# A feed-forward stage in seven products: two weight buffers and four hidden buffers swap roles, and the low part of each weight form is made in one VectorE operation

## The chip, the cores and the metric

The kernel runs on one core of one Trainium2 chip. The metric is the device time in microseconds (us) of one execution. All times of the stages come from one profiled execution of the kernel before.

## What is computed

One layer of a hybrid decoder trunk on 512 positions of width 1024: a mixer (a gMLP group and a Mamba-2 group behind one input projection), a feed-forward part, a gated embedding, and a last RMSNorm. The change is in the feed-forward part alone.

```
hid = jax.nn.relu(rmsnorm(h, norm_mlp_g[i]) @ w_ff1[i])
h = h + (hid * hid) @ w_ff2[i]
gate = jax.nn.sigmoid(rmsnorm(h, ple_norm_g[i]) @ w_ple_gate[i])
h = h + gate * (p[i] @ w_ple_proj[i])
```

w_ff1 is 1024 x 4096 and w_ff2 4096 x 1024, all in fp32.

## The kernel before

**Stages.** The input projection and the two mixers run until about 265 us, the output projection and the embedding product until 366 us, the feed-forward part from 366 to 694 us, and the gate and the last norm to the end at 749 us. Each engine has a program of its own, written out in order, and waits on semaphores; nothing reorders it.

**Seven products for eight.** The feed-forward part is cut into four units, u = 0 to 3, each of 1024 hidden columns. In a unit each of the two matrix products is made block-wise by a Strassen-like scheme with seven products instead of eight (m = 0 for w_ff1, m = 1 for w_ff2). The right-hand factor of a product is a *form* of the weights: one of the four 512 x 512 blocks B11, B12, B21, B22 of a unit's weights, or a sum or difference of blocks, T1 to T4. The left-hand factor is a block of the activations (A11, A12, A21, A22) or a sum of them (S1 to S4). TensorE takes the 14 forms of a unit in the order of `FIRST` (B11, B21, T2, T3, T4, T1, B22) and `SECOND` (B11, T3, T2, B21, B22, T1, T4). The text calls them form 0 to form 13 of the unit; form 9 is T2 with S2, form 10 is B21 with A12. The next unit's form 0 is B11 and its form 1 is B21.

**Two parts of each number.** A float32 value is split into a high part and a low part of type fp32r, and each product is three matmuls (`product`, lines 1645 to 1647). For the weights ScalarE copies a form into the high half of a ring buffer (`split_form`, L762), and VectorE subtracts it from the form for the low half (`split_form`, L1403). Both work in two steps of 128 x 1024, called half 0 and half 1 here. The ring has three buffers, so ScalarE may write form n only when TensorE has ended form n-3.

**Where the forms come from.** Four SBUF buffers, `quarter` 0 to 3, hold the forms one after another (`QUARTER`). SP loads blocks from HBM into them (`load_quarter`, L510; `reload_b12`, L518). GpSimd (POOL) issues DMAs that add to what a quarter holds (`t_add`, L642): T3 is the B12 in the quarter plus B22 read from HBM, T2 is the B11 in its quarter plus T3, T4 is the B21 in its quarter plus T2, and for m = 1 T1 is a B12 loaded once more plus B11 from HBM. For m = 0 VectorE makes T1 from two quarters (`make_t1`, L1444). B12, T3 and T1 live in quarter 0, B11 and T2 in quarter 1, B21 and T4 in quarter 2, B22 in quarter 3. A block may be loaded when the last form made in its quarter has its low part, and T4, which reads T2's quarter, has landed.

**The hidden activations.** VectorE joins the seven products of m = 0 into the four blocks of the hidden matrix (`combine`, L1459), ScalarE applies relu and square (`hidden`, L773 and L775), VectorE forms S1 to S4 (`s_add`, L1474), and both engines split them (`split_a`, L794 and L1481). Several of these tiles share memory: the high part of S2 is written where that of A11 was, and S2 itself where the low part of A11 was. The products of m = 1 are added to the residual h by VectorE (`h_add`, L1498). Form 10 starts when the sum of form 8 ("T3 above") is out of its PSUM banks, and form 1 of the next unit starts when the sum of form 13 ("T4") is; VectorE makes that last sum behind the low parts of the next unit's forms 0 and 1:

```
                if u:
                    h_add(u - 1, "T4")
                both(2)
```

## Time and profile before

| what | value |
|---|---|
| median of 3 runs | 748.88 us (748.5 to 749.48) |
| time of the profiled execution | 751.16 us |
| its span, first to last instruction | 749.4 us |
| TensorE busy with matmuls | 728.0 us, 97% |
| VectorE busy | 528.3 us, 71% |
| ScalarE busy | 410.8 us, 55% |
| mean granted TensorE clock | 0.993 of full |

The profiled execution's time is 1.8 us more than its span and 2.3 us more than the median of the runs. Matmuls overlap each other in the records, so a busy share near 100% does not say that TensorE loses nothing. What it loses is read from the starts of its matmuls: a form is as long as the distance from its first matmul to the first of the next form.

### The profile page before, as it was taken

The page shows a single profiled execution, that of the slowest core. Times are in us where ns is not written, and L with a number is a line of the kernel's source. Part 1 is how long each engine was busy: PE and PEld are TensorE (multiplying, and loading weights), DVE is VectorE, ACT ScalarE, POOL GpSimd, SP SyncE. Part 2 cuts the span into 40 slices and gives each one's busy share as a digit, 9 for nine tenths or more (in the row PEclk, how much of TensorE's full clock was granted, in tenths as well). Part 3 has the DMA queues.
Part 4 walks back from the last instruction along what each step waited for, and adds up shares of the span by engine and source line. Part 5 has one row for each costly group of instructions (what it writes and reads, how often), then busy time and mean ns, then how long its engine had stood idle before and what let it go on. Part 6 is the DMA issues. An engine that isn't in the chain of part 4 may idle for free.

```text
span 749.4 us, 9989 instructions
## 1 busy us (share of the span) xinstructions
PE 728.0 (97%) x3972; PEld 624.5 (83%) x3972; DVE 528.3 (71%) x553; ACT 410.8 (55%) x521; POOL 134.0 (18%) x112
## 2 busy tenths in 40 slices
PE   7999999999999999999999899989999999999996
PEld 7888877878878888888999689978999789978784
DVE  5546794576667465556787976879487956799774
ACT  5534456644674833315764733675356726483875
POOL 1021000766455000000102211122102220220000
PEclk9999999999999999999999999999999999999998
DMA  9633222342241163137839988789959896987311
GB/s 334 185 105 85 84 85 87 129 152 85 88 162 61 57 217 120 57 113 197 225 115 211 207 231 168 207 169 264 217 176 205 200 258 163 216 182 270 112 57 57
DMA packets 53381, 118.24 MB, mean 158 GB/s; under 512 B 5052, under 2 KB 6744, under 8 KB 53336
## 3 DMA queue, kind: packets, MB, share of 16 engines
q1 hardware_dynamic: 40968, 84.03, 34.5%
q0 software_dynamic: 11136, 29.36, 21.5%
q10 hardware_dynamic: 1232, 4.23, 1.8%
q8 instruction: 31, 0.51, 0.3%
q14 instruction: 14, 0.11, 0.0%
HBM read 96.60 MB, written 4.23 MB: 135 GB/s over the span
## 4 chain that ended last, share of the span: by engine, by line
PE 59%; DVE 16%; DMA 13%; issue 7%; ACT 4%; POOL 1%; DVEq 0%; ACTq 0%; SPq 0%; POOLq 0%
PE acc L1645 17%; PE acc L1647 16%; PE acc L1646 16%; DMA quarter<-in_w_ff 8%; DVE ring_lo L1403 7%; DMA quarter<-quarter 4%; PE side L1710 3%; DVE h L1498 2%; PE side L1807 2%; DVE fS_lo L1481 2%; ACT ring_hi L762 2%; DVE fA_lo L1481 1%; PE side L1774 1%; DVE fA_raw L1459 1%; PE side L1814 1%
## 5 line engine op out<-in xcount | busy, mean ns | idle before, releaser
L1403 DVE TENSOR_TENSOR ring_lo<-quarter,ring_hi 128x1024 fp32r<-128x1024 f32 x112 | 132.9, 1220 | 64.0 <-ACT ring_hi L762 64.0
L762 ACT ACTIVATE ring_hi<-quarter 128x1024 fp32r<-128x1024 f32 x112 | 113.7, 1050 | 99.5 <-DMA quarter<-in_w_ff 52.6
L1645 PE MATMUL acc<-w_hi,a_hi 128*128 128x512 f32 x256 | 104.4, 408 | 0.0
L1647 PE MATMUL acc<-w_hi,a_lo 128*128 128x512 f32 x256 | 100.1, 391 | 0.0
L1646 PE MATMUL acc<-w_lo,a_hi 128*128 128x512 f32 x256 | 99.7, 390 | 0.0
L642 POOL DMA_DIRECT2D quarter<-in_w_ff x24 | 29.2, 1219 | 265.0 <-DMA quarter<-in_w_ff 264.8
L1646 PE MATMUL acc<-xS_lo,ring_hi 128*128 128x256 f32 x256 | 72.4, 283 | 0.0
L1100 DVE TENSOR_TENSOR w_lo<-w_raw,w_hi 128x1024 fp32r<-128x1024 f32 x36 | 48.1, 1338 | 28.1 <-ACT w_hi L663 27.8
L1645 PEld LDWEIGHTS acc<-w_hi,a_hi 128*128 128x128 f32 x256 | 48.1, 188 | 10.8 <-issue 1.4
L1646 PEld LDWEIGHTS acc<-w_lo,a_hi 128*128 128x128 f32 x256 | 48.2, 188 | 10.7 <-issue 1.4
L1647 PEld LDWEIGHTS acc<-w_hi,a_lo 128*128 128x128 f32 x256 | 48.0, 188 | 10.4
L1645 PE MATMUL acc<-xS_hi,ring_hi 128*128 128x256 f32 x192 | 54.4, 283 | 0.6 <-issue 0.6
L1647 PE MATMUL acc<-xS_hi,ring_lo 128*128 128x256 f32 x192 | 54.3, 283 | 0.0
L1646 PE MATMUL acc<-xA_lo,ring_hi 128*128 128x256 f32 x192 | 54.3, 283 | 0.0
L1647 PE MATMUL acc<-xA_hi,ring_lo 128*128 128x256 f32 x192 | 54.3, 283 | 0.0
L1645 PE MATMUL acc<-xA_hi,ring_hi 128*128 128x256 f32 x192 | 54.3, 283 | 0.0
L1646 PEld LDWEIGHTS acc<-xS_lo,ring_hi 128*128 128x128 f32 x256 | 49.1, 192 | 0.0
L663 ACT ACTIVATE w_hi<-w_raw 128x1024 fp32r<-128x1024 f32 (+1 forms) x40 | 39.9, 1006 | 16.0 <-PE acc L1647 13.7
L1645 PE MATMUL acc<-ring_hi,fA_S_hi 128*128 128x512 f32 x96 | 38.7, 403 | 9.3 <-DVE fS_lo L1481 7.7
L642 POOL DMA_DIRECT2D quarter<-quarter x32 | 28.0, 874 | 106.3 <-DMA quarter<-in_w_ff 61.1
L1196 DVE SCALAR_TENSOR_TENSOR h<-acc,m_rstd,h 128x1024 f32<-128x1024 f32 x16 | 20.5, 1284 | 32.5 <-PE acc L1647 32.5
L1645 PE MATMUL acc<-a_hi,w_hi 128*128 128x512 f32 x96 | 38.9, 406 | 0.0
(274 smaller groups left out, 1825.2 us busy)
## 6 DMA issues: line engine op xcount, KB each, us to landing
quarter<-in_w_ff SPq DMA_DIRECT2D x72, 512.0 KB, 5.0
w_raw<-in_w_in SPq DMA_DIRECT2D x36, 512.0 KB, 3.7
quarter<-quarter POOLq DMA_DIRECT2D x32, 512.0 KB, 5.2
quarter<-in_w_ff POOLq DMA_DIRECT2D x24, 512.0 KB, 9.8
w_raw<-in_w_out SPq DMA_DIRECT2D x16, 512.0 KB, 3.4
h<-in_x SPq DMA_DIRECT2D x8, 512.0 KB, 4.4
seg<-cs_dram ACTq DMA_DIRECT2D x8, 512.0 KB, 3.9
w_raw<-in_w_ple_gate SPq DMA_DIRECT2D x8, 512.0 KB, 4.5
```

Of the source, the lines that this page charges most:

```text
L642: pool.dma_start(quarter[QUARTER[name]][at], src, accum_op=ALU.add).then_inc(t_landed[QUARTER[name]][p], 16)
L663: act.activation(w_hi[:, half, at, :], w_raw[:, p, 0:n, :], ACT.Copy, scale=scale).then_inc(hi_ready, 1)
L762: act.activation(ring[n % 3][0][at], quarter[i][at], ACT.Copy).then_inc(form_hi, 1)
L1100: ins = dve.tensor_tensor(lo, raw, hi, ALU.subtract)
L1196: dve.scalar_tensor_tensor(hs, acc[:, i:i + 2, :], m_rstd[:, c:c + 1], hs, ALU.mult, ALU.add).then_inc(dve_evac, 1)
L1403: dve.tensor_tensor(lo[at], src, hi[at].bitcast(F32), ALU.subtract).then_inc(form_lo, 1)
L1481: dve.tensor_tensor(f_lo[name][:], f_raw[name][:], f_hi[name][:].bitcast(F32), ALU.subtract).then_inc(hid_lo, 1)
L1498: dve.tensor_tensor(hq, hq, bank, op).then_inc(h_added, 1)
L1645: pe.matmul(dst, st[0], mv[0], start=start, stop=False)
L1646: pe.matmul(dst, st[0], mv[1], start=False, stop=False)
L1647: return pe.matmul(dst, st[1], mv[0], start=False, stop=stop)
L1710: ins = pe.transpose(bank[:, i * P:i * P + P], src(i), ident[:])
```

## The change

The kernel changes in four ways, all in the feed-forward part.

1. *Weight buffers.* A function `home(m, name)` takes the place of `QUARTER`: for m = 0 B12, T3 and T1 live in quarter 0 and B11 and T2 in quarter 1, as before; for m = 1 these two exchange their quarters. So the B12 of m = 1 is loaded into quarter 1, where m = 0 had T2, and the B11 of m = 1 into quarter 0, where m = 0 had T1. The next unit's B12 goes where m = 1 had T2, its B11 where m = 1 had T1. SP's order changes with it: B12, B21, B11, B22 for m = 1 and B12, B11, B22, B21 for m = 0.
2. *Hidden buffers.* The high parts of A11 and A12 share one tile, and those of S2 and S1; the low parts of A11 and A12 share one; S2 has memory of its own. The waits follow: the high part of A12 waits for the end of form 7, that of S1 for the end of form 9, and S2 no longer waits for form 7.
3. *Order.* ScalarE splits A12 behind S2 and S4. VectorE makes the sum for form 5 ("U3") before the low part of A11, makes S2 ahead of the low part of form 9, and the low parts of A12 and S4 behind the two sums of T3. In unit 0 two sums within h move ahead of S4.
4. *One operation.* VectorE makes the low part of a form in one operation on 128 x 2048 that waits for both halves of the high part and signals both at its end.

```diff
@@ -23,7 +23,16 @@
...
 SECOND_A = ("A11", "S3", "S2", "A12", "S4", "S1", "A22")
-QUARTER = {"T3": 0, "T1": 0, "B12": 0, "B11": 1, "T2": 1, "B21": 2, "T4": 2, "B22": 3}
+
+
+def home(m, name):
+
+    return {"B12": m, "T3": m, "T1": m, "B11": 1 - m, "T2": 1 - m, "B21": 2, "T4": 2, "B22": 3}[name]
+
+
+LOADS = ((("B12", 0), ("B11", 1)), (("B11", 0), ("B12", 1)), (("B21", 0), ("B21", 1)), (("B22", 0), ("B22", 1)))
+SUMMED = ((("T3", 0), ("T2", 1)), (("T2", 0), ("T3", 1), ("T1", 1)), (("T4", 0), ("T4", 1)))
+RELOAD = 1
 
@@ -112,10 +121,8 @@
...
         f_hi, f_lo, f_raw = {}, {}, {}
-        with ExitStack() as early:
-            f_lo["A11"] = sb("fA11_lo", [P, 4, 256], F32R, where=early)
+        f_lo["A11"] = f_lo["A12"] = sb("fA11_A12_lo", [P, 4, 256], F32R)
         f_raw["S2"], f_lo["S2"] = raw_lo("fS2")
-        f_lo["A12"] = sb("fA12_lo", [P, 4, 256], F32R)
         f_raw["S3"], f_lo["S3"] = raw_lo("fS3")
@@ -146,8 +153,8 @@
...
             ple = sb("ple", [P, NS, D], where=early)
-        f_hi["A11"] = f_hi["S2"] = sb("fA11_S2_hi", [P, 4, 256], F32R)
-        f_hi["A12"] = f_hi["S1"] = sb("fA12_S1_hi", [P, 4, 256], F32R)
+        f_hi["A11"] = f_hi["A12"] = sb("fA11_A12_hi", [P, 4, 256], F32R)
+        f_hi["S2"] = f_hi["S1"] = sb("fS2_S1_hi", [P, 4, 256], F32R)
         f_hi["A22"] = sb("fA22_hi", [P, 4, 256], F32R)
@@ -483,19 +490,19 @@
...
 
-                i = QUARTER[name]
+                i = home(m, name)
                 row, col = int(name[1]) - 1, int(name[2]) - 1
...
                     if m:
-                        last_use = {"B12": "T1", "B11": "T2", "B22": "B22", "B21": "T4"}[name]
+                        last_use = ("T1", "T2", "T4", "B22")[i]
                         sp.wait_ge(form_lo, form_count(u, 0, last_use, p))
-                        if name == "B11":
+                        if i == 1:
                             sum_landed(sp, u, 0, "T4", p)
...
                     elif u:
-                        last_use = {"B12": "T1", "B11": "T2", "B22": "B22", "B21": "T4"}[name]
+                        last_use = ("T2", "T1", "T4", "B22")[i]
                         sp.wait_ge(form_lo, form_count(u - 1, 1, last_use, p))
-                        if name == "B11":
+                        if i == 0:
                             sum_landed(sp, u - 1, 1, "T4", p)
@@ -526,23 +533,23 @@
...
             for u in range(UNITS):
+                load_quarter(u, 1, "B12")
+                load_quarter(u, 1, "B21")
                 load_quarter(u, 1, "B11")
-                load_quarter(u, 1, "B21")
-                load_quarter(u, 1, "B12")
                 load_quarter(u, 1, "B22")
...
                 if u < UNITS - 1:
+                    load_quarter(u + 1, 0, "B12")
                     load_quarter(u + 1, 0, "B11")
-                    load_quarter(u + 1, 0, "B12")
                     load_quarter(u + 1, 0, "B22")
...
             last = UNITS - 1
-            sp.wait_ge(ff_step, product_end(last, 1, "T2"))
+            sp.wait_ge(ff_step, product_end(last, 1, "B21"))
             load_gain(a["final_norm_g"], 0)
             for p in range(4):
-                sp.wait_ge(form_lo, form_count(last, 1, "T1" if p < 2 else "T2", 1))
-                if p >= 2:
+                sp.wait_ge(form_lo, form_count(last, 1, "T2" if p < 2 else "T1", 1))
+                if p < 2:
                     for i in range(2):
@@ -630,17 +637,17 @@
...
                     pool.wait_ge(form_lo, form_count(u, m, "B11", p))
-                    src = quarter[0][at]
+                    src = quarter[home(m, "T3")][at]
                 elif name == "T1":
-                    pool.wait_ge(q_landed[0][p], 16 * (3 * u + 3))
+                    pool.wait_ge(q_landed[RELOAD][p], 16 * (3 * u + 3))
                     k = 8 * u + 2 * p
...
                     pool.wait_ge(form_lo, form_count(u, m, "B21", p))
-                    src = quarter[1][at]
-                pool.dma_start(quarter[QUARTER[name]][at], src, accum_op=ALU.add
-                               ).then_inc(t_landed[QUARTER[name]][p], 16)
+                    src = quarter[home(m, "T2")][at]
+                pool.dma_start(quarter[home(m, name)][at], src, accum_op=ALU.add
+                               ).then_inc(t_landed[home(m, name)][p], 16)
 
@@ -781,14 +788,14 @@
...
                             act.wait_ge(ple_stored[s], 16)
+                    elif name == "A12":
+                        act.wait_ge(ff_step, product_end(u, 1, "B11"))
+                        act.wait_ge(hid_lo, lo_count(u, "A11"))
                 else:
                     act.wait_ge(s_raw, s_count(u, name))
-                    if name == "S2":
-                        act.wait_ge(ff_step, product_end(u, 1, "B11"))
-                        act.wait_ge(hid_lo, lo_count(u, "A11"))
-                    elif name == "S1":
-                        act.wait_ge(ff_step, product_end(u, 1, "B21"))
-                        act.wait_ge(hid_lo, lo_count(u, "A12"))
+                    if name == "S1":
+                        act.wait_ge(ff_step, product_end(u, 1, "T2"))
+                        act.wait_ge(hid_lo, lo_count(u, "S2"))
                     elif name == "S4":
@@ -1018,10 +1025,10 @@
...
                 hidden(u, "A12")
-                split_a(u, "A12")
                 split_a(u, "S2")
...
                 split_a(u, "S4")
+                split_a(u, "A12")
                 both(11)
@@ -1394,13 +1401,12 @@
...
 
-            def split_form(n, p):
-
-                at = (slice(None), slice(2 * p, 2 * p + 2))
+            def split_form(n):
+
                 hi, lo = ring[n % 3]
-                src = quarter[QUARTER[form_of(n)[2]]][at]
-                dve.wait_ge(form_hi, 2 * n + p + 1)
-                dve.tensor_tensor(lo[at], src, hi[at].bitcast(F32), ALU.subtract).then_inc(form_lo, 1)
+                dve.wait_ge(form_hi, 2 * n + 2)
+                dve.tensor_tensor(lo[:], quarter[home(*form_of(n)[1:])][:], hi[:].bitcast(F32), ALU.subtract
+                                  ).then_inc(form_lo, 2)
 
@@ -1467,7 +1472,6 @@
...
                     dve.wait_ge(s_raw, s_count(u, "S1"))
-                    dve.wait_ge(ff_step, product_end(u, 1, "B11"))
                 else:
@@ -1542,12 +1544,12 @@
...
                     x_split("S1")
+                both(5)
+                combine(u, "U3")
                 split_a(u, "A11")
-                both(5)
+                both(6)
                 if u == 0:
                     x_split("S4")
-                combine(u, "U3")
-                both(6)
                 combine(u, "C21")
@@ -1557,20 +1559,20 @@
...
                 s_add(u, "S1")
+                s_add(u, "S2")
                 both(9)
-                s_add(u, "S2")
-                s_add(u, "S4")
-                split_a(u, "S2")
-                both(10)
-                split_a(u, "A12")
                 if u == 0:
...
                     dve.tensor_tensor(h12, h12, h22, ALU.subtract).then_inc(h_added, 1)
+                s_add(u, "S4")
+                split_a(u, "S2")
+                both(10)
                 h_add(u, "T3 right")
                 h_add(u, "T3 above")
+                split_a(u, "A12")
+                split_a(u, "S4")
                 both(11)
-                split_a(u, "S4")
                 h_add(u, "T2")
```

The other places follow from these: `quarter_count` and `sum_landed` count by the new homes, `t_add` and ScalarE's `split_form` take the quarter from `home`, and the calls of VectorE's `split_form` lose their loop over the halves.

SP's DMA issues from the end of unit 1's second half to the start of the next unit, before (L510 is `load_quarter`, L518 `reload_b12`; in_w_ff1 is w_ff1; t_landed2 counts T4):

```order
52 L510 DMA quarter0<-in_w_ff2 128x2x512 [waits form_lo] x2
53 L510 DMA quarter3<-in_w_ff2 128x2x512 [waits form_lo] x2
54 L518 DMA quarter0<-in_w_ff2 128x2x512 [waits form_lo,t_landed10]
55 L518 DMA quarter0<-in_w_ff2 128x2x512 [waits form_lo,t_landed11]
56 L510 DMA quarter1<-in_w_ff1 128x2x512 [waits t_landed20,form_lo]
57 L510 DMA quarter1<-in_w_ff1 128x2x512 [waits t_landed21,form_lo]
58 L510 DMA quarter0<-in_w_ff1 128x2x512 [waits form_lo] x2
59 L510 DMA quarter3<-in_w_ff1 128x2x512 [waits form_lo] x2
60 L510 DMA quarter2<-in_w_ff1 128x2x512 [waits form_lo] x2
```

And now:

```order
52 L517 DMA quarter0<-in_w_ff2 128x2x512 [waits form_lo] x2
53 L517 DMA quarter3<-in_w_ff2 128x2x512 [waits form_lo] x2
54 L525 DMA quarter1<-in_w_ff2 128x2x512 [waits form_lo,t_landed00]
55 L525 DMA quarter1<-in_w_ff2 128x2x512 [waits form_lo,t_landed01]
56 L517 DMA quarter0<-in_w_ff1 128x2x512 [waits t_landed20,form_lo]
57 L517 DMA quarter0<-in_w_ff1 128x2x512 [waits t_landed21,form_lo]
58 L517 DMA quarter1<-in_w_ff1 128x2x512 [waits form_lo] x2
59 L517 DMA quarter3<-in_w_ff1 128x2x512 [waits form_lo] x2
60 L517 DMA quarter2<-in_w_ff1 128x2x512 [waits form_lo] x2
```

Rows 56 and 57 load the next unit's first block as soon as T4 has landed. That was B11, and is now B12, on which T3's addition waits; B11 comes behind it, after the low part of form 12. B21 (row 60) stays last.

VectorE's operations from the low part of form 9 to that of form 11 in units 1 to 3, before:

```order
L1403 TENSOR_TENSOR ring_lo<-quarter,ring_hi 128x1024 [waits form_hi] x2
L1474 TENSOR_TENSOR fS_raw<-fA_S_raw,fS_raw 128x1024 [waits ff_step,s_raw]
L1474 TENSOR_TENSOR fS_raw<-fA_raw,fS_raw 128x1024 [waits hid_raw,s_raw]
L1481 TENSOR_TENSOR fS_lo<-fS_raw,fA_S_hi 128x1024 [waits s_raw,hid_hi]
L1403 TENSOR_TENSOR ring_lo<-quarter,ring_hi 128x1024 [waits form_hi] x2
L1481 TENSOR_TENSOR fA_lo<-fA_raw,fA_S_hi 128x1024 [waits hid_hi]
L1498 TENSOR_TENSOR h<-h,acc 128x2x512 [waits h_added,ff_step] x2
L1403 TENSOR_TENSOR ring_lo<-quarter,ring_hi 128x1024 [waits form_hi] x2
```

And now, here from the making of S2 on (numbers of buffers are shown):

```order
311 L1478 TENSOR_TENSOR fS2_raw<-fA11_S4_raw,fS1_raw 128x1024 [waits s_raw]
312 L1408 TENSOR_TENSOR ring2_lo<-quarter0,ring2_hi 128x2048 [waits form_hi]
313 L1478 TENSOR_TENSOR fS4_raw<-fA12_raw,fS2_raw 128x1024 [waits hid_raw,s_raw]
314 L1485 TENSOR_TENSOR fS2_lo<-fS2_raw,fS2_S1_hi 128x1024 [waits s_raw,hid_hi]
315 L1408 TENSOR_TENSOR ring0_lo<-quarter2,ring0_hi 128x2048 [waits form_hi]
316 L1502 TENSOR_TENSOR h<-h,acc 128x2x512 [waits h_added,ff_step] x2
317 L1485 TENSOR_TENSOR fA11_A12_lo<-fA12_raw,fA11_A12_hi 128x1024 [waits hid_hi]
318 L1485 TENSOR_TENSOR fS4_lo<-fS4_raw,fA11_S4_hi 128x1024 [waits hid_hi]
319 L1408 TENSOR_TENSOR ring1_lo<-quarter3,ring1_hi 128x2048 [waits form_hi]
```

S2 stands ahead of form 9's low part, the low part of A12 behind the two sums, and each low part of a form is one row of 2048 columns.

## Rows read from the trace of the kernel before

**Rows 1.** Units 0 to 3: stretch, PE, PEld, DVE, ACT, POOL, clock, DMA share, GB/s
```profile
366.00:451.06 85.06, 80.87 (x506) 72.65 (x504) 69.62 (x61) 48.32 (x49) 12.50 (x12) 0.98 0.79 197
451.06:532.43 81.37, 78.96 (x505) 71.70 (x504) 62.64 (x55) 43.70 (x44) 13.75 (x15) 1.00 0.86 207
532.43:613.12 80.69, 79.00 (x506) 71.70 (x504) 62.52 (x54) 44.61 (x45) 14.09 (x15) 1.00 0.87 209
613.12:693.70 80.58, 78.95 (x508) 71.51 (x507) 66.41 (x60) 44.13 (x49) 11.61 (x12) 1.00 0.82 204
```

**Rows 2.** TensorE's timeline: first matmuls of forms (start, length, name, idle before)
```profile
420.83 0.50 PE L1645 MATMUL acc<-ring_hi,fA_S_hi 128*128 128x512 f32 x1 [2.53 <-DVE fS_lo L1481]
429.21 0.47 PE L1645 MATMUL acc<-ring_hi,fA_S_hi 128*128 128x512 f32 x1 [1.06 <-issue]
...
504.68 0.50 PE L1645 MATMUL acc<-ring_hi,fA_S_hi 128*128 128x512 f32 x1 [2.24 <-DVE fS_lo L1481]
510.59 0.47 PE L1645 MATMUL acc<-ring_hi,fA_S_hi 128*128 128x512 f32 x1 [0.17 <-issue]
...
532.43 0.28 PE L1645 MATMUL acc<-xA_hi,ring_hi 128*128 128x256 f32 x1
538.18 0.28 PE L1645 MATMUL acc<-xA_hi,ring_hi 128*128 128x256 f32 x1
```

**Rows 3.** Chain that ended last, piece before unit 1's form 9
```profile
482.57 10.27 DMA quarter<-in_w_ff
493.13 5.08 DMA quarter<-quarter
...
502.33 1.05 ACT fA_S_hi L794
503.40 1.22 DVE fS_lo L1481
```

**Rows 4.** Instructions by line and form
```profile
L1403 DVE TENSOR_TENSOR ring_lo<-quarter,ring_hi 128x1024 fp32r<-128x1024 f32 x112 | 132.9, 1220 | 64.0 <-ACT ring_hi L762 64.0
L1616 DVE TENSOR_TENSOR y<-y,conv 128x512 f32<-128x512 f32 x8 | 5.5, 691 | 9.4 <-ACT conv L1058 9.4
```

**Rows 5.** VectorE's timeline: one pair of halves, the sum of T4
```profile
519.48 2.35 DVE L1403 TENSOR_TENSOR ring_lo<-quarter,ring_hi 128x1024 fp32r<-128x1024 f32 x2
...
535.12 1.21 DVE L1498 TENSOR_TENSOR h<-h,acc 128x1024 f32<-128x1024 f32 x1
```

**Rows 6.** ScalarE's timeline: form 1's half 1 behind its load
```profile
532.88 1.06 ACT L762 ACTIVATE ring_hi<-quarter 128x1024 fp32r<-128x1024 f32 x1 [2.90 <-DMA quarter<-in_w_ff]
```

**Rows 7.** GpSimd's timeline: additions T3 (m = 1, half 0), T2 (half 0), next unit's T3
```profile
480.34 1.21 POOL L642 DMA_DIRECT2D quarter<-in_w_ff  x1 [20.70 <-DMA quarter<-in_w_ff]
...
490.60 0.90 POOL L642 DMA_DIRECT2D quarter<-quarter  x1 [6.82 <-DMA quarter<-in_w_ff]
...
521.60 1.21 POOL L642 DMA_DIRECT2D quarter<-in_w_ff  x1 [13.27 <-DMA quarter<-in_w_ff]
```

**Rows 8.** SP's queue: loads of B12 (m = 1), then the next unit's B11 and B21
```profile
476.19 1.50 SPq L510 DMA_DIRECT2D quarter<-in_w_ff  x2
...
513.24 0.37 SPq L510 DMA_DIRECT2D quarter<-in_w_ff  x1
...
521.86 0.37 SPq L510 DMA_DIRECT2D quarter<-in_w_ff  x1
```

**Rows 9.** DMA queues (packets, MB, share), windows 519 to 525, 505 to 509, 444 to 449
```profile
q1 hardware_dynamic: 1075, 2.08, 101.8%
...
q0 software_dynamic: 407, 0.80, 111.6%
...
q0 software_dynamic: 324, 0.63, 69.1%
q1 hardware_dynamic: 329, 0.64, 38.8%
```

**Rows 10.** Unit 0's form 9: stretch, busy times, clock
```profile
420.83:429.21 8.38, 7.31 (x24) 5.60 (x25) 8.17 (x8) 5.10 (x7) 1.76 (x2) 0.80 1.11 204
```

29 lines of the change are left out of this document (13 added, 16 removed).

## The prediction

> **What bounds the kernel now.** I read the busy time by stage first [rows 1]: the reader is to see that TensorE works through all four feed-forward units at a granted clock of 0.98 to 1.00, that no other engine is busy for more than 85% of a unit, and that the units are not equally long. TensorE's timeline gives the length of a form that waits for nothing [rows 2]: 538.18 - 532.43 = 5.75 us in the first half of a unit, and (532.43 - 510.59) / 4 = 5.46 us in the second. Seven of each are 78.5 us. The units last 85.1, 81.4, 80.7 and 80.6 us [rows 1], so TensorE loses 6.6, 2.9, 2.2 and 2.1 us in them. That 13.8 us is all that can be won in this stage by removing waits. Everything behind 693.7 us is code that the change doesn't move, and I cost it at nothing: its weight load waits on the low parts of the same two last forms as before.
>
> Where the loss lies is in the same rows. Form 9 (T2 with S2) of unit 1 begins 2.24 us late and is 510.59 - 504.68 = 5.91 us long instead of 5.46; unit 0's begins 2.53 us late. Form 10 follows with 1.06 and 0.17 us [rows 2]. Units 2 and 3 repeat unit 1, with 1.5 us before form 9. The chain of waits says what is late [rows 3]: T3's addition (10.27 us), T2's addition (5.08 us, landed at 498.21), then on ScalarE the high part of T2, relu and square of A12 and the high part of S2, and the low part of S2 on VectorE. TensorE starts 0.06 us after that ends, at 504.62. Before form 1 of a unit stands another chain, which loses nothing yet: B21's second half lands at 532.88, ScalarE takes 1.06 us [rows 6], VectorE the low part and at 535.12 to 536.33 the sum of T4, for which TensorE needs the banks [rows 5]. Form 1 starts at 538.18: slack 1.85 us.
>
> **What the change takes away.** (a) T3 and T2 of m = 1. B12's load goes to the quarter whose last user is T2 instead of T1, some 10 us earlier, so T3 leaves the chain. T2 then waits for the other addend: B11 is loaded when T1's low part is ready (477.3) and its low part is made about 9 us later. I put T2's second half at 496.8 against 498.2, a gain of 1.4 us, and no more. (b) ScalarE splits A12 behind S2, so one operation of 1.05 us [rows 3] leaves the chain. Together S2's low part is ready at about 504.6 - 2.1 = 502.5 us. Without a wait form 9 would begin at 504.68 - 2.24 = 502.44. About 0.1 to 0.3 us is left, and form 9 gets its 5.46 us back. Units 1 to 3 lose 2.9 + 2.2 + 2.1 = 7.2 us now; I leave them 0.3 us each: **6.3 us** gained.
>
> (c) Unit 0. Its form 9 took 8.38 us at a granted clock of 0.80 [rows 10]; less the 1.06 us that form 10 waited for and the normal 5.46 this is 1.9 us lost to the clock. The two sums within h now stand ahead of S4 and S2's low part on VectorE: 2 x 1.14 us are added ahead of it, which eats most of (a) and (b) there. I keep 1.5 us of the 2.53 us, and give form 4 a wait of 1.4 us: the merged low parts of forms 3 and 4, fed half by half from HBM, each begin 1.1 us later. With 0.3 us for form 10 that is 3.2 us lost instead of 6.6: **3.4 us** gained, with ends 0 (the clock falls again) and 5.
>
> **What the merged operation does.** A pair of halves takes 2.35 us [rows 5]. One operation of 2048 columns isn't in the trace. From 512 to 1024 columns the time grows from 691 to 1220 ns [rows 4], so 2048 take about 1220 + 2 x 529 = 2278 ns; the other end is two operations, 2.44 us. 56 forms save between 4 and, at worst, lose 5 us of VectorE's time; with VectorE 77% busy in the stage [rows 1] none of it is on the path. What is on it is the start: half 0's low part used to be made while half 1 was still on ScalarE or under way, so wherever the halves come apart the low part ends 2.28 - 1.23 = 1.05 us later. Form 1 of a unit is such a place. That costs its slack of 1.85 us 1.05 us and no time by itself.
>
> **What the new order of loads adds.** Here I see the price. At each of the three unit boundaries SP used to load B11, then B12, B22, B21. Now B12 goes first, into the place that T4 has freed. All of this is about 2.1 us earlier than in the trace, since form 9 waits no longer: B12's first half is issued at 513.24 - 2.1 = 511.1 [rows 8] and lands 4.1 us later, as the load of 476.19 did, after which its addition was issued at 480.34 [rows 7, 8]. So T3's additions are issued at 515.1 and 517.6 and not at 521.60. They move packets from 4.4 us after their issue. Behind B12 SP has B11, B22 and B21 still to load, six halves of 0.52 MB, the first issued at 515.3, when form 12's low part is ready, the last at 520.5, behind form 13's.
>
> The queues' rates [rows 9]: SP's queue alone 2.08 MB in 6 us, 0.347 MB/us; the additions' queue alone 0.80 MB in 4 us, 0.20 MB/us; both together 0.63 and 0.64 MB in 5 us, 0.127 MB/us each. From 516.7 to 519.7 SP moves 1.04 MB alone. The remaining 2.1 MB share with T3's additions (1.05 MB, to 528.0), and 1.05 MB of loads is still open then. Before, T3 was issued 6 us later, and the loads were nearly through. If nothing follows, the last 1.05 MB takes 3.0 us, and with 1.2 us for completion B21 is there at 532.1. But T2's first half may start as soon as T3's first half has landed, and form 0's low part is made by then; so the additions' queue doesn't pause, and the rest goes at 0.127: 8.3 us, landed at 537.4. That B21 doesn't leave SP's queue earlier, since it is last there, makes it the one that pays. From its landing it is 1.06 + 2.28 + 1.2 = 4.6 us to the end of the T4 sum. Form 1 is due at 538.18 - 2.24 - 0.45 - 0.17 = 535.3 us. The wait is 532.1 + 4.6 - 535.3 = 1.4 us at least and 6.7 at most by these rates. A T2 addition moves SBUF to SBUF, for which no row shows the rate beside loads; if loads got 0.1 MB/us beside it, B21 would land at 539.6, with 8.9 us of wait. Between 1.4 and 8.9 I take **5.2 us, three times: 15.6 us**. Ends for all three: 4 and 27 us.
>
> **Sum.** 15.6 - 6.3 - 3.4 = +5.9 us on the profiled execution's 751.16 us: 757.1. That execution stands 2.3 us above the median of the runs, so the median should become 748.88 + 5.9 = **754.8 us**. With 4 us for the boundaries the sum is -5.7 (743), with 20 us (6.7 each) +10.3 (759), with 27 us +17 (766).
>
> **Rivals.** *Faster: the transfers don't collide.* If T2 gets out of the way, or loads keep most of their 0.347 MB/us beside an addition, B21 lands before 530.7 and nothing waits; the gains of 9.7 us stand alone: 739.2 us. For it: the shared rate of 0.127 comes from one stretch of 5 us, in which SP may simply have had little to issue; the share of 38.8% that q1's packets took there says that its engines weren't full [rows 9]. Against: B21's halves were last to land already, 11.0 us after the issue of 521.86 [rows 6, 8]. The point from which it decides is B21's second half landing 1.4 us before my lower end.
>
> *Faster, weaker, or no change.* The boundaries cost 3 x 2.5 to 3 x 3.7 us and cancel the gains: 747 to 750.4 us.
>
> *Slower by the clock.* Form 9 of unit 0 shows that a wait of 2.53 us was followed by a granted clock of 0.80 and cost 1.9 us more than the wait [rows 10]; unit 1's wait of 2.24 us was followed by 1.00 [rows 1, 2]. If waits of 5.2 us at the three boundaries each bring such a stretch, the sum is 5.9 + 3 x 1.9 = +11.6: 760.5 us. 0.80 is a mean between the two levels of 1.2 and 2.4 GHz.
> The Trainium skill, "TensorE: Matmul & The Clock Gate", section "What's actually happening", has the clock throttled by default and released by activity, which speaks for this case after any long pause.
>
> *Slower: T2 of m = 0 comes late.* If B21's and T2's delay reaches form 2 and form 4, another 1.9 us per boundary is lost behind the 5.2: about the same 760.5 us.
>
> *The change doesn't do what it says.* If B11's late load keeps T2 of m = 1 where it was, only the split of A12 helps: 1.05 us in each of three units instead of 2.1. The sum is 3.2 us higher: 758.
>
> **How the numbers follow.** A measurement can tell about 0.2%, 1.5 us, from no change. Chances: the forecast, with a wait for B21 above 3.7 us at the boundaries, 0.56; T2 of m = 1 not relieved 0.04; clock or T2 of m = 0 on top 0.08; no collision or a weak one 0.24; cancelled within 1.5 us 0.08. The likeliest case's own range is 750.5 to 763. So faster 0.24, same 0.08, slower 0.68. The range takes in the middle of the faster cases and ends where 7% lie above: 741 to 763.
>
> **What would show it.** In the profile after: form 9 waits under 0.5 us in units 1 to 3; the rows of L1408 have 2278 ns; T3's addition for the next unit is issued near 515, some 6 us earlier; B21's second half lands at 534 to 538 and is what ScalarE waits for, up to 8 us; form 1 starts behind the sum of T4 with 4 to 7 us of idle time. The prediction is wrong if form 1 waits under 2 us, if the clock in the first half of units 1 to 3 falls under 0.9, or if form 9 still waits for S2.

## The result, and the profile after

The changed kernel takes 752.78 us in the median of 20 runs, the kernel before 748.41 us in the median of 20 runs on the same chips: the ratio is 1.0056, with a 95% interval from 1.0043 to 1.0069. By the ratio it is slower by 4.2 us (the two medians are 4.4 us apart); 5.9 us were forecast. Single executions differ much more than those of the kernel before (748.18 to 756.43 us against 745.8 to 749.63), and the text below comes back to that. The profiled execution shown here took 752.03 us.

The page's first part, and the line of the merged operation, of the kernel after:

```profile
span 750.0 us, 9985 instructions
...
PE 727.4 (97%) x3972; PEld 624.5 (83%) x3972; DVE 524.1 (70%) x497; ACT 410.9 (55%) x521; POOL 134.3 (18%) x112
...
L1408 DVE TENSOR_TENSOR ring_lo<-quarter,ring_hi 128x2048 fp32r<-128x2048 f32 x56 | 128.0, 2288 | 67.9 <-ACT ring_hi L769 67.9
```

VectorE has 4.2 us less work than in the kernel before, as worked out; one low part takes 2288 ns (2278 were expected). That tells nothing of the time. The lengths of the units do (columns as in [rows 1]):

```profile
364.41:446.59 82.18, 79.23 (x505) 71.74 (x504) 68.87 (x48) 47.45 (x48) 14.00 (x14) 1.00 0.83 210
446.59:528.67 82.08, 79.51 (x506) 71.79 (x505) 61.30 (x40) 43.70 (x44) 14.59 (x15) 1.00 0.84 205
528.67:608.97 80.30, 79.12 (x505) 71.87 (x504) 61.30 (x40) 43.69 (x44) 13.47 (x13) 1.00 0.85 209
608.97:694.45 85.48, 80.42 (x509) 73.49 (x508) 66.83 (x48) 46.05 (x50) 11.02 (x11) 0.96 0.75 194
```

Beside [rows 1], unit 0 is 3.0 us shorter (its form 0 began at 365.84 in the kernel before; the window in [rows 1] begins 0.16 us later), unit 1 is 0.7 us longer, unit 2 0.4 us shorter, unit 3 4.9 us longer. The stage lasts 330.0 us instead of 327.9. That is 2.1 us more in the stage. The profiled executions differ by only 0.9 us, since the one of before came to the stage 1.4 us later; its granted clock was 0.97 in the first 50 us and that of the one after 1.00:

```profile
0.00:50.00 50.00, 46.15 (x229) 39.60 (x230) 26.44 (x34) 25.47 (x40) 5.04 (x13) 0.97 0.69 223
```

```profile
0.00:50.00 50.00, 46.71 (x235) 39.66 (x236) 26.88 (x35) 26.35 (x40) 6.39 (x14) 1.00 0.69 223
```

The first is of the kernel before, the second of the one after. TensorE's timeline of the kernel after has the waits themselves; they stand beside [rows 2]:

```profile
389.23 0.35 PE L1647 MATMUL acc<-xA_hi,ring_hi 128*128 128x256 f32 x1 [1.63 <-issue]
418.89 0.50 PE L1647 MATMUL acc<-ring_hi,fS_S_hi 128*128 128x512 f32 x1 [1.25 <-DVE fS_lo L1485]
453.46 0.38 PE L1647 MATMUL acc<-xA_hi,ring_hi 128*128 128x256 f32 x1 [0.96 <-DVE h L1502]
500.98 0.50 PE L1647 MATMUL acc<-ring_hi,fS_S_hi 128*128 128x512 f32 x1 [1.32 <-DVE fS_lo L1485]
535.54 0.39 PE L1647 MATMUL acc<-xA_hi,ring_hi 128*128 128x256 f32 x1 [0.96 <-DVE h L1502]
553.29 0.39 PE L1647 MATMUL acc<-xA_hi,ring_hi 128*128 128x256 f32 x1 [0.22 <-DVE fA_raw L1464]
619.94 0.58 PE L1647 MATMUL acc<-xA_hi,ring_hi 128*128 128x256 f32 x1 [5.06 <-DVE h L1502]
```

The number in brackets is the idle time in front of the matmul. Where the text says that a wait is counted from the starts of the forms, it is the distance between the first matmuls of two forms less that of forms that wait for nothing (5.76 us in the first half of a unit, 5.44 us in the second); it comes out 0.15 to 0.3 us longer.

Three things are to be seen. Form 9's wait is gone in units 2 and 3 (no row), and is 1.25 us in unit 0 and 1.32 us in unit 1. Form 1 of units 1 to 3 (453.46, 535.54, 619.94) now waits for the sum of T4 (L1502), 0.96, 0.96 and 5.06 us. And form 4 waits: 1.63 us in unit 0 (389.23), 0.22 us in unit 2, and 0.23 us in unit 1.

The form behind the longest of these waits is itself too long, 7.60 us from 619.94 to 627.54 instead of 5.76. No wait lies in it; its granted clock is 0.74 (columns as in [rows 1]):

```profile
619.94:627.54 7.60, 7.60 (x49) 7.60 (x49) 6.71 (x4) 1.12 (x2) 1.10 (x2) 0.74 0.79 155
```

That is 1.84 us more. What the expectations below call time before form 2 is this: form 1 at a lower clock.

Why the wait at the third boundary is five times as long as at the others is in ScalarE's and GpSimd's timelines. The boundary of units 1 and 2 (form 0 at 528.67), ScalarE's high parts of form 0's half 1 and form 1's two halves, then GpSimd's two T2 additions:

```profile
522.62 1.06 ACT L769 ACTIVATE ring_hi<-quarter 128x1024 fp32r<-128x1024 f32 x1 [3.45 <-DMA quarter<-in_w_ff]
529.65 1.06 ACT L769 ACTIVATE ring_hi<-quarter 128x1024 fp32r<-128x1024 f32 x1 [5.97 <-DMA quarter<-in_w_ff]
530.90 1.06 ACT L769 ACTIVATE ring_hi<-quarter 128x1024 fp32r<-128x1024 f32 x1 [0.20 <-DMA quarter<-in_w_ff]
...
526.65 1.79 POOL L649 DMA_DIRECT2D quarter<-quarter  x2 [9.67 <-DVE ring_lo L1408]
```

And that of units 2 and 3 (form 0 at 608.97), with T3's additions in front:

```profile
601.72 1.06 ACT L769 ACTIVATE ring_hi<-quarter 128x1024 fp32r<-128x1024 f32 x1 [0.73 <-DMA quarter<-in_w_ff]
611.47 1.06 ACT L769 ACTIVATE ring_hi<-quarter 128x1024 fp32r<-128x1024 f32 x1 [8.69 <-DMA quarter<-in_w_ff]
615.31 2.00 ACT L769 ACTIVATE ring_hi<-quarter 128x1024 fp32r<-128x1024 f32 x2 [2.78 <-DMA quarter<-in_w_ff]
...
593.93 1.23 POOL L649 DMA_DIRECT2D quarter<-in_w_ff  x1 [8.17 <-DMA quarter<-in_w_ff]
595.80 1.22 POOL L649 DMA_DIRECT2D quarter<-in_w_ff  x1 [0.64 <-DMA quarter<-in_w_ff]
605.75 0.90 POOL L649 DMA_DIRECT2D quarter<-quarter  x1 [8.73 <-DVE ring_lo L1408]
609.45 0.86 POOL L649 DMA_DIRECT2D quarter<-quarter  x1 [2.79 <-DMA quarter<-in_w_ff]
```

At the second boundary form 0's half 1 came 6.0 us before the form, its long low part ended at 526.07, and T2's additions, which wait for that (the releaser is ring_lo), were issued 2.0 us before form 0. B21 was nearly through by then: its halves are taken up at 1.0 and 2.2 us after form 0's start. At the third, B11's half 1 came 7.2 us before form 0 and T2's first addition went out 3.2 us before it, T2's second only 0.5 us behind form 0, when T3's second half had landed. B21's halves came 2.5 and 6.3 us after form 0's start. So B21 either gets through before T2's packets or waits beside them, and 1.2 us in T2's issue parts the two cases here. That the spread between executions comes from this is likely, and not shown: one execution was profiled.

The DMA queues in that stretch (packets, MB, share), windows 601 to 605 (T3 beside loads), 609 to 611 (T2 beside loads) and 611 to 613:

```profile
q0 software_dynamic: 272, 0.52, 70.7%
q1 hardware_dynamic: 272, 0.52, 39.5%
...
q0 software_dynamic: 89, 0.36, 91.2%
q1 hardware_dynamic: 82, 0.14, 18.9%
...
q0 software_dynamic: 115, 0.41, 104.5%
q1 hardware_dynamic: 10, 0.02, 2.6%
```

Beside T3's additions the loads had 0.13 MB/us, as in [rows 9]. Beside T2's they had 0.07 MB/us, in about as many packets as T2 (82, of which 12 are under 512 bytes, and 89), and a load's packet carries half as much as one of T2. In the last window they had 0.01 MB/us; those 10 packets are among the last of B21's half 1.

### The profile page after: what moved, and what is told of

It is laid out like the page before. It is cut to its first block, busy times and chain, and to the rows that moved or that the text cites. A ratio compares the mean times of both kernels' runs of the same rounds, so it can differ in the third digit from the quotient of the medians.

```text
span 750.0 us, 9985 instructions
## 1 busy us (share of the span) xinstructions
PE 727.4 (97%) x3972; PEld 624.5 (83%) x3972; DVE 524.1 (70%) x497; ACT 410.9 (55%) x521; POOL 134.3 (18%) x112
## 4 chain that ended last, share of the span: by engine, by line
PE 70%; DVE 11%; DMA 10%; issue 6%; ACT 2%; SPq 0%; POOL 0%; DVEq 0%; ACTq 0%; POOLq 0%
PE acc L1647 20%; PE acc L1649 20%; PE acc L1648 20%; DMA quarter<-in_w_ff 7%; DVE ring_lo L1408 4%; PE side L1712 3%; DMA quarter<-quarter 2%; PE side L1809 2%; DVE h L1502 1%; DVE fA_raw L1464 1%; DVE fS_raw L1478 1%; ACT ring_hi L769 1%; DVE fS_lo L1485 1%; PE side L1776 1%; PE side L1816 1%
## 5 line engine op out<-in xcount | busy, mean ns | idle before, releaser
L1408 DVE TENSOR_TENSOR ring_lo<-quarter,ring_hi 128x2048 fp32r<-128x2048 f32 x56 | 128.0, 2288 | 67.9 <-ACT ring_hi L769 67.9
L1647 PEld LDWEIGHTS acc<-xA_hi,ring_hi 128*128 128x128 f32 x192 | 37.6, 196 | 10.4 <-DVE h L1502 7.6
```

Of the source, the lines that this page charges most:

```text
L1408: dve.tensor_tensor(lo[:], quarter[home(*form_of(n)[1:])][:], hi[:].bitcast(F32), ALU.subtract).then_inc(form_lo, 2)
L1647: pe.matmul(dst, st[0], mv[0], start=start, stop=False)
```

## The experiments

Twelve kernels, in three groups of four; each group shared its runs of the kernel before. Q is the theory that B21 lands late because additions and loads share the DMA engines at the unit boundary. Its rivals put the loss on the merged operation (M), call that operation neutral (N), or take the exchange of quarters for the gain (H). Intervals of two experiments in different groups are compared through their ratios.

**1. The changed kernel with half operations.** Part 4 undone:

```diff
-                dve.wait_ge(form_hi, 2 * n + 2)
-                dve.tensor_tensor(lo[:], quarter[home(*form_of(n)[1:])][:], hi[:].bitcast(F32), ALU.subtract
-                                  ).then_inc(form_lo, 2)
+                for p in range(2):
+                    at = (slice(None), slice(2 * p, 2 * p + 2))
+                    dve.wait_ge(form_hi, 2 * n + p + 1)
+                    dve.tensor_tensor(lo[at], quarter[home(*form_of(n)[1:])][at], hi[at].bitcast(F32), ALU.subtract
+                                      ).then_inc(form_lo, 1)
```

> The changed kernel with one part undone: the low part of a form is again made half by half. Theory Q (the queues: B21 lands late because T3's additions run beside the loads, and the merged operation only adds 1.05 us to whatever waits for a second half): form 1 of units 1 to 3 begins about 1 us earlier, form 4's waits (1.8, 0.4 and 0.4 us in the profile after) go, unit 3's wait for B21 stays at some 4 us: 3 to 5 us less than the changed kernel, so about 749. Theory M (the merged operation is the whole cause, roles and order are a gain of 6 to 9 us): about 741. Theory N (the operation is neutral, since it also saves 0.07 us 56 times): 752 to 753.

752.86 us, ratio 1.0057 (1.0034 to 1.0080): the same as with the merge. The number is N's; the profile is not. Form 4's waits went, as Q had said, but form 1's became longer at two boundaries: 3.1, 2.5 and 4.5 us by the starts of the forms, against 1.1, 1.1 and 5.2 us, and at the first and third boundary form 1 then ran at 0.79 and 0.71 and lost 1.4 and 2.05 us more. With half operations T2's first addition is issued 6 to 7.5 us before form 0, since it needs only half of form 0's low part, and B21's second half lands 4.8 to 6.8 us behind form 0 at every boundary. The merge had held T2 back (to 1.8 and 2.0 us before form 0) and so let B21 through at two boundaries. Two effects of 4 us each cancel in these profiles: the boundaries cost 13.6 us instead of 9.3, waits and clock, and forms 4 and 9 wait 4.0 us less.

**2. The kernel before with the merge alone.** The same operation in the code before.

> The kernel before with the merged low part alone. Theory Q: form 1's slack of 1.85 us takes up its 1.05 us, form 9 is not reached by it, unit 0's form 4 loses some 1 us: 1 to 4 us slower than before, 750 to 752. Theory M: the merge alone costs as much as the whole change and more, since nothing is gained at form 9: 10 us or more, over 758. Theory N: within 1 us of before.

765.93 us, ratio 1.0247 (1.0220 to 1.0274), 18 us slower. Q (750 to 752) and N are refuted, and I had this step wrong by far. M's number is right and its reason is half right. The units, in the kernel before with the merge (columns as in [rows 1]):

```profile
365.89:454.23 88.34, 81.41 (x505) 72.90 (x504) 69.19 (x48) 48.51 (x49) 13.14 (x13) 0.98 0.77 194
454.23:538.77 84.54, 79.79 (x505) 71.73 (x504) 61.60 (x40) 43.81 (x44) 13.97 (x15) 1.00 0.83 201
538.77:623.89 85.12, 80.83 (x505) 72.86 (x504) 61.60 (x40) 43.69 (x44) 14.82 (x15) 0.98 0.83 199
623.89:708.77 84.88, 81.14 (x509) 72.81 (x508) 66.80 (x48) 45.18 (x49) 10.96 (x11) 0.98 0.76 193
```

Each unit is 3 to 4.5 us longer than in [rows 1], 15 us in all in this profile (the profiled execution of before was itself 2.3 us above its median), and only 1.0 us of that is the wait of form 1. Form 9 waits in all four units, but it did so before: by the starts of the forms 2.75 us in each, against 2.8, 2.4, 1.7 and 1.6 us, which is 2.5 us more. Form 9 itself and the wait behind it take 3.5 us more, mostly because its clock is now 0.77 and 0.76 in units 2 and 3 too. Form 8 waits 0.5 to 0.9 us, 2.9 us in all. The largest part, 4.8 us, stands before form 4 (1.8, 0.9, 1.5 and 0.6 us), which had waited for nothing. It waits for the sum U, which VectorE makes behind form 4's low part. Unit 2's form 4, unit 1's form 9 and form 10, and what VectorE did ahead of form 9:

```profile
563.28 0.39 PE L1641 MATMUL acc<-xA_hi,ring_hi 128*128 128x256 f32 x1 [1.31 <-DVE fA_raw L1457]
...
510.48 0.50 PE L1641 MATMUL acc<-ring_hi,fA_S_hi 128*128 128x512 f32 x1 [2.46 <-DVE fS_lo L1479]
516.91 0.47 PE L1641 MATMUL acc<-ring_hi,fA_S_hi 128*128 128x512 f32 x1 [0.69 <-issue]
```

```profile
498.80 2.29 DVE L1402 TENSOR_TENSOR ring_lo<-quarter,ring_hi 128x2048 fp32r<-128x2048 f32 x1 [5.43 <-ACT ring_hi L762]
501.01 1.22 DVE L1479 TENSOR_TENSOR fS_lo<-fS_raw,fS_hi 128x1024 fp32r<-128x1024 f32 x1
502.15 1.22 DVE L1457 TENSOR_TENSOR fA_raw<-fA_raw,acc 128x1024 f32<-128x1024 f32 x1
503.28 1.22 DVE L1472 TENSOR_TENSOR fS_raw<-fS_raw,fA_raw 128x1024 f32<-128x1024 f32 x1
504.42 2.29 DVE L1402 TENSOR_TENSOR ring_lo<-quarter,ring_hi 128x2048 fp32r<-128x2048 f32 x1
506.62 1.22 DVE L1472 TENSOR_TENSOR fS_raw<-fA_S_raw,fS_raw 128x1024 f32<-128x1024 f32 x1
507.87 1.23 DVE L1472 TENSOR_TENSOR fS_raw<-fA_raw,fS_raw 128x1024 f32<-128x1024 f32 x1
509.20 1.23 DVE L1479 TENSOR_TENSOR fS_lo<-fS_raw,fA_S_hi 128x1024 fp32r<-128x1024 f32 x1
```

VectorE idles 5.4 us for form 8's second high part, which comes when T3's half 1 has landed, and then works through eight operations without a gap to the low part of S2, for which TensorE waits. Half of form 8's low part used to be made in that idle time; in one operation it all comes behind it. The 5.43 us of idle time is no slack at all. At form 4 it is the same: VectorE idles 4.2 us for the high part and then owes the whole low part before U.

**3. B21 ahead of B22.** The changed kernel with two lines exchanged:

```diff
-                    load_quarter(u + 1, 0, "B22")
                     load_quarter(u + 1, 0, "B21")
+                    load_quarter(u + 1, 0, "B22")
```

> The changed kernel, but SP loads the next unit's B21 ahead of its B22 (B22 is first wanted for T1, some 12 us later). Nothing else moves. Theory Q: 1.05 MB less stand ahead of B21 in SP's queue, so it lands 3 to 8 us earlier, unit 3's wait of 5.1 us and the 1.1 us of the others go or shrink to the issue of B21 (it still waits for form 13's low part): 4 to 7 us faster than the changed kernel, 746 to 749. Theory M: B21's landing is not what counts, the low part's late start is: within 1 us of the changed kernel.

750.57 us, ratio 1.0032 (1.0013 to 1.0051). B21's second half was taken up 0.2 and 0.4 us before form 0's start and 0.4 us behind it (2.2 to 6.3 us behind it in the kernel after), and form 1 waited 0, 0.06 and 0 us. At the boundary Q's mechanism is shown and M's is refuted. The time is not Q's 746 to 749: only about 2 us came out, and the interval touches that of the changed kernel (1.0043 to 1.0069). Form 4 now waited 1.75 to 1.85 us in every unit. At the second boundary form 0 waited too, 1.5 us for its own low part (1.7 by the starts), since B11's second half landed only 3.6 us before form 0, beside T3's additions:

```profile
531.01 0.36 PE L1647 MATMUL acc<-xA_hi,ring_hi 128*128 128x256 f32 x1 [1.51 <-DVE ring_lo L1408]
...
556.17 0.39 PE L1647 MATMUL acc<-xA_hi,ring_hi 128*128 128x256 f32 x1 [1.60 <-DVE fA_raw L1464]
```

**4. B11 ahead of B12, as before the change.** The two other lines of the same list exchanged.

> The changed kernel, but SP loads the next unit's B11 ahead of its B12, as before the change. B11 waits for form 12's low part, so B12 and with it T3's additions come about 4 us later, beside fewer loads. Theory Q: form 1 no longer waits for B21 (0 to 0.5 us instead of 1.1, 1.1 and 5.1); T2 comes later, and form 2 may wait up to 2 us: 2 to 5 us faster than the changed kernel. Theory M: form 1's wait stays at about 1 us, and the later T2 makes it slower: 0 to 5 us slower than the changed kernel.

754.85 us, ratio 1.0102 (1.0072 to 1.0132), 3 us slower than the change: M's number, and against Q's 2 to 5 us faster. B11 has to wait for form 12's low part, and B12 and all the loads stand behind it. T3 was issued only 7 to 8 us before form 0. Form 1's waits were 2.3, 1.1 and 0 us, form 2's up to 1.4 us (unit 3), and form 4 waited 1.85 us in units 1 to 3. The boundaries did cost less, as Q has it, and form 4 took back more, which neither theory had; it is the wrong place to delay T3.

**5. Part 1 alone.** The kernel before with the exchanged quarters and SP's new order.

> The kernel before with part 1 of the change alone: quarters 0 and 1 exchanged for m = 1, and SP's new order. Hidden buffers, order and half operations as before. Theory Q (the early T3 of the next unit delays B21): form 1 waits as in the changed kernel with halves (3.1, 2.5 and 4.5 us and 3.5 us before form 2), while form 9's waits shrink by some 1.4 us each, from T2's earlier landing: 4 to 10 us slower than before, 752 to 758. Theory H (the exchange is the gain and what costs is the order or the merge): 743 to 745.

749.71 us, ratio 1.0011 (0.9993 to 1.0029): no change, and neither Q's 752 to 758 nor H's 743 to 745. In its profile form 9 waits for nothing in any unit (8.5 us won by the starts of the forms; form 10 of unit 0 waits 1.6 us). T2's second half landed 5.3 us before form 8 of unit 1, where it had landed 1.4 us behind it. Form 1 waits 0, 2.5 and 3.8 us and then loses 0, 1.6 and 2.5 us to a clock of 0.77 and 0.67. Gain and loss are both there, each where it was expected, the gain larger than the 1.4 us for each unit that Q had; their sum is near nothing.

**6. Parts 2 and 3 alone.** Hidden buffers and order.

> The kernel before with parts 2 and 3 alone: hidden buffers and the order on ScalarE and VectorE, quarters and half operations as before. Theory Q: ScalarE has one operation of 1.05 us less in front of S2, no load moves, so form 9 waits 1 us less in each of four units and form 1 still waits for nothing: 3 to 5 us faster than before, 743 to 745. Theory H: the order of this part brings nothing or costs (the two sums ahead of S4 in unit 0, A12 and S4 later): within 1 us of before or up to 3 us slower.

745.68 us, ratio 0.9966 (0.9952 to 0.9980), 2.5 us faster, a little short of Q's 3 to 5. In units 1 to 3 form 9 waited 1.0, 0.6 and 0.5 us instead of 2.4, 1.7 and 1.6, counted from the starts of the forms; in unit 0 3.6 us instead of 2.8, with 1.76 us more at a clock of 0.76 behind it. No wait at the boundaries, as Q expects.

**7. Parts 2, 3 and 4 without part 1.**

> Parts 2, 3 and 4 without part 1: the quarters as before. The merge alone cost 18 us in the old order, with form 9 waiting 2.75 us in every unit because S2 was made behind form 9's long low part. Theory S (the new order, with S2 ahead of it, is what makes the merge bearable): most of those 18 us go, form 9 waits 1.5 us or less, form 4 some 1 to 1.8 us: 749 to 755. Rival (it is the exchange of quarters, which brings T3 and T2 earlier, that makes it bearable): form 9 waits 2.5 us and more, and the time stays over 758.

761.06 us, ratio 1.0167 (1.0151 to 1.0182). The rival stands, S falls: form 9 waits 2.3 to 2.5 us in units 1 to 3 and 5.0 us in unit 0. Parts 2 and 3 give back 6 us of the 18, no more, and 2.5 us of these they give without the merge too. The exchange of quarters, with its earlier T3 and T2, is what the merge needs.

The changed kernel and experiments 1, 2, 5, 6 and 7 as a table of parts (ratio to before, and what that is in us of 748):

| parts | ratio | us |
|---|---|---|
| 1 | 1.0011 | +0.8 |
| 2 and 3 | 0.9966 | -2.5 |
| 1, 2 and 3 | 1.0057 | +4.3 |
| 4 | 1.0247 | +18.5 |
| 2, 3 and 4 | 1.0167 | +12.5 |
| all | 1.0056 | +4.2 |

**8. U ahead of form 4's low part.** In the kernel after VectorE makes the sum U behind the low part of form 4, and TensorE needs the banks that U reads.

```diff
                 combine(u, "C11")
+                combine(u, "U")
                 both(4)
                 if u == 0:
                     x_split("A22")
-                combine(u, "U")
```

> The changed kernel with VectorE's sum U made ahead of the low part of form 4 and not behind it (VectorE is idle for 4.2 us there). If form 4's waits (1.79, 0.39 and 0.37 us in the profile after, 1.8 us in every unit where B21 goes first) are waits for U behind the merged low part, they go entirely, and the time falls by 1.5 to 3 us, to 750 or 751. Rival: what ends just before form 4 is the high part of T4, and U only ends with it: the wait stays and the time is that of the changed kernel within 1 us. Should the boundary take back what form 4 gives (form 1's due time comes earlier by it, the transfers don't), the waits before form 4 go and the time stays at 752 too, with longer waits before form 1.

752.00 us, ratio 1.0052 (1.0036 to 1.0068). Form 4's waits fell from 1.79, 0.39 and 0.38 us to 0.61, 0 and 0, by the starts of the forms. The time stayed, as the expectation has it for the case that the boundary takes it back, but the profile doesn't show that: form 1 waited 0.95, 1.6 and 3.7 us in it, 6.2 us in all beside the 7.4 us of the kernel after, and this profile's stage is 2.9 us shorter. One profile of each doesn't settle it, and why the median stayed is open.

**9. Both repairs on the merged kernel.** B21 first and U early.

> The changed kernel with both repairs: U ahead of the low part of form 4, and B21 loaded ahead of B22. With B21 first alone, form 1's waits were 0, 0.06 and 0 us and form 4's 1.75 to 1.85 us in every unit (7.2 us in all). Theory Q with U: form 1 still waits for nothing, form 4's waits go, except where T4's own low part is late: 4 to 6 us faster than with B21 first alone, 745 to 747, and so faster than the kernel before by 2 to 4 us. Rival (a boundary of fixed transfers: whatever is won ahead of it is lost at it): 750 to 751 as with B21 first alone.

749.78 us, ratio 1.0022 (1.0010 to 1.0035): near the rival's 750, and not Q's 745 to 747. Form 1 waits for nothing, but form 4 still 0.6 to 0.8 us, in units 1 to 3 for T4's merged low part, form 9 0.8 to 1.7 us, and form 0 of unit 1 1.9 us for its own merged low part. In units 1 to 3 the merged low part, or work of VectorE behind it, is next in line where one wait is removed.

**10. Half operations with B21 first.** The edits of 1 and 3 together.

> The changed kernel with half operations and with B21 loaded ahead of B22. With halves alone the boundaries cost 3.1, 2.5 and 4.5 us before form 1 and 3.5 us before form 2, of 16 us lost in the stage. Theory Q: B21 is through before T2's additions start, those 13.6 us shrink to under 3, nothing else is changed: 8 to 11 us faster than with halves alone, 742 to 745, and 4 us or more faster than the kernel before. Rival: T2's additions are delayed by B21's in turn, and form 2 waits instead of form 1: 748 to 751.

741.15 us, ratio 0.9917 (0.9894 to 0.9940): 6.2 us faster than before, some 10 us faster than either the change or experiment 1. The units (columns as in [rows 1]):

```profile
365.69:446.14 80.45, 79.06 (x506) 71.70 (x504) 69.75 (x61) 49.55 (x50) 13.20 (x13) 1.00 0.83 211
446.14:525.83 79.69, 79.00 (x506) 71.70 (x504) 62.84 (x56) 43.99 (x45) 14.40 (x15) 1.00 0.86 210
525.83:604.25 78.42, 78.42 (x506) 71.85 (x504) 62.54 (x54) 43.10 (x43) 14.28 (x14) 1.00 0.89 213
604.25:683.29 79.04, 78.92 (x509) 71.53 (x508) 66.47 (x60) 45.21 (x49) 10.07 (x10) 1.00 0.80 209
```

Unit 2 is TensorE's work and nothing else. Against experiment 1, one exchanged pair of lines took away 13.6 us at the boundaries, waits and the lower clock behind them. T2's first addition is still issued 5 to 7 us before form 0, but B21 is ahead of B22: its second half is taken up 0.9 and 1.2 us before form 0, and 0.5 us behind it at the third boundary.

**11. The same, and unit 0's two sums within h later.** They stand behind form 10's low part instead of ahead of S4.

> As the one with halves and B21 first, and in unit 0 the two sums within h stand behind the low part of form 10 and no longer ahead of S4. If they are what delays S2's low part before form 9 of unit 0 (1.47 us of wait with halves, 3.58 us in the kernel with the new order and the old quarters), that wait falls by some 1 to 2 us and the time with it: 1 to 2 us under the kernel with halves and B21 first. Rival (form 9 of unit 0 waits for S2's high part behind T2, as in the other units): no difference.

740.67 us, ratio 0.9895 (0.9878 to 0.9913), the lowest of all, and not to be told from the one before it; the 1 to 2 us were not found. The wait before form 9 of unit 0 went from 1.47 us to 0 as expected, and the time didn't follow: form 10 waits instead.

```profile
423.12 0.50 PE L1649 MATMUL acc<-ring_hi,fA_A_hi 128*128 128x512 f32 x1 [1.92 <-DVE fA_A_lo L1487]
```

**12. The same move in the kernel of experiment 6.**

> Parts 2 and 3 of the change alone (quarters and halves as before), with the two sums of unit 0 behind the low part of form 10. In the run without this move unit 0's form 9 waited 3.58 us and lost 1.76 us more, the only place where it did worse than the kernel before. Expected: the wait falls to about 1.5 us, 1.5 to 3.5 us faster than parts 2 and 3 alone (745.7), so 742 to 744. Rival (the wait is T2's landing, not the sums): 745 to 746.

745.59 us, ratio 0.9966 (0.9951 to 0.9981), no difference to experiment 6. The number is the rival's, and its reason is not: the two sums did hold form 9, whose wait of 3.6 us fell to 1.2. But form 10 now waits 2.6 us, and runs at 0.76 behind that, 1.7 us longer. VectorE is behind there in unit 0; the order chooses which form waits.

## Why the prediction was right, and where its steps were not

The direction, and the place that decides it, were right: the gain at form 9 was real, and the next unit's B21, last in SP's queue behind earlier additions, took back more. Experiments 3 and 10 show it by taking away nothing but B22 from in front of B21. How near the number came is partly luck. In the two profiles the stage grew by 2.1 us, where the same sum gave 5.9: the boundaries cost 9.5 us instead of 15.6, the gains were 8.2 instead of 9.7, and one wait wasn't in the sum.

*The signs that the prediction had named* came out mixed. For it: T3's addition for unit 2 was issued at 513.2 (near 515 had been named), the low part took 2288 ns, form 1 waits behind the sum of T4. Against it: B21's second half landed at 530.9 there and not at 534 to 538, form 1 waited under 2 us at two boundaries of three, and form 9 of unit 1 still waited for S2, 1.32 us. The clock of unit 3's first half was 0.93, over the 0.9 that had been named, with 0.74 in form 1.

*Form 9, units 1 to 3: 6.3 us forecast.* The waits before forms 9 to 11 went from 7.4 us to 2.2 us, counted from the starts of the forms: 5.2 us. In unit 1 form 9 still waited 1.32 us, where at most 0.3 was expected. The term of T2, "a gain of 1.4 us, and no more", was too small: against form 8 T2's second half landed 1.2 us earlier in unit 1, 2.5 in unit 2 and 5.0 in unit 3. The merge takes part of this back: with half operations (experiment 1) form 9 waits in unit 0 alone, 1.5 us.

*Unit 0: 3.4 us forecast, 3.0 measured.* Its form 9 waited 1.25 us (1.5 kept in the sum), form 4 1.63 us (1.4 in the sum), and its clock was 1.00.

*The boundaries: 3 x 5.2 us forecast.* Measured in this profile 1.2, 1.2 and 7.1 us, the last with 1.84 us of lower clock, together 9.5 us: inside the stated 4 to 27. The wait at the third boundary, 5.2 us by the starts of the forms, is the middle value; the two others are under the lower end of 1.4. The prediction had T3 14.4 us ahead of form 0's due time (515.1 and 529.5), and T3 is issued 15.0 to 15.5 us before form 0. What it missed is the switch: T2 may go behind or ahead of B21, and there is little in between. The third boundary is the upper case, 6.3 us from form 0 to B21's second half, where the 535.9 that goes with its 5.2 us is 6.4 us behind its form 0; the others are the lower case, 2.2 us, where its 532.1 is 2.6 us behind. The 1.2 us for completion in that sum is shown by no run: in the trace of before B21's second half landed 0.5 us behind the end of its last data packet. Nor do the first packets of T3 come 4.4 us after the issue there, but 4.7 us (521.60 and 526.29).

*Form 4, 0.39 and 0.38 us in units 1 and 2,* wasn't in the sum outside unit 0. The stage comes to 9.5 + 0.8 - 5.2 - 3.0 = +2.1 us, which is what the two profiles show. The ratio says +4.2; single executions of the changed kernel lie up to 8 us apart, and I take the rest for boundaries that fell the other way. No profile of a slower execution was taken of it, so that is argued and not shown.

*The merged operation is the step that failed.* The prediction had its later start, 1.05 us, but charged it in two places only: to form 1's slack, at no cost, and to form 4 of unit 0. Alone it costs 18 us, with parts 2 and 3 15 us (experiment 7 against 6), with all the other parts and B21 first 8 or 9 us (experiments 3 and 9 against 10), and with all the other parts and B21 last nothing (the change against experiment 1). Its length was right to 10 ns. What was wrong is to look for the delay at form 1 and to leave the rest to an average, VectorE 77% busy. An average says nothing of a place where VectorE idles for an input and then owes several operations in a row, and experiment 2 shows such places at form 4 and at form 8. It was neutral in the change because there it cost only 4.0 us, at forms 4 and 9, and the delay it adds also held T2 back, which spared 4.3 us at the boundaries (experiment 1, one profile of each). That 5.9 us came near 4.2 owes something to this: two sizes, of the boundary without and with the merge, were not told apart.

*The shares of the queues.* The sum went by one stretch in which T3 and loads had equal parts, 0.127 MB/us each, and put 0.1 MB/us as an outer value beside T2. Measured beside T2: 0.07 MB/us. The Trainium skill, "DMA: Bandwidth & Descriptors", section "Queues, rings and completion order", says that a DMA engine takes packets from its queues in turn. The trace agrees in its first two windows, with 272 and 272 packets beside T3 and 89 and 82 beside T2, so the queue with the larger packets gets the larger part of the bytes; the 115 and 10 packets of the third don't show it. By its rule the wait would be 6.5 us, as the prediction worked out; the third boundary had 5.2 us. The prediction says that no row shows T2 beside loads. The trace of before does, at its first boundary, window 450.2 to 452.9, where T2 ran beside the last packets of B21:

```profile
q0 software_dynamic: 176, 0.45, 87.8%
q1 hardware_dynamic: 50, 0.08, 9.6%
```

The loads had 0.03 MB/us there, far under the outer value of 0.1, and B21's second half landed 12.4 us after its issue instead of 11.0 us.

*The clock rival* came true at one boundary of three: 1.84 us behind a wait of 5.06 us, where 1.9 us had been worked out from unit 0 of the kernel before. The waits of 0.96 us left the clock at 1.00.

## What to carry to other kernels

A wait that is removed moves everything behind it earlier, except transfers that hang on a queue's order: before counting a gain, write down for the next joint of the loop what stands in each DMA queue ahead of the first tile wanted, and put tiles in the order in which they are wanted. Merging operations saved 0.07 us per pair here and gave up the overlap with a producer that delivers in halves (1.05 us at each place where the halves come apart). Look for the places where the engine idles for that producer and a consumer waits for what comes behind: there the delay can be on the path, whatever the engine's average load. And a part of a change that measures as neutral may be a large loss beside a large gain: here each shows only when the other is gone.
